# A decoder layer on one Trainium2 core: expert tiles in one pipeline instead of pairs, second norm two tiles behind

## The chip, the cores and the metric

The kernel runs on one core of a Trainium2 chip. The metric is the device time of one execution in microseconds (us). The engines are TensorE (PE; its weight loads are PEld), VectorE (DVE), ScalarE (ACT), GpSimd (POOL) and SyncE (SP, which only issues DMAs here). GpSimd issues the indirect DMAs, that gather or scatter rows by a list of row numbers; they go through a queue of their own, q0, beside the weight loads of SyncE in q1. All share the core's 16 DMA engines.

## What is computed

One layer over 576 tokens (a prompt of 512 and 8 x 8 samples) of width 1024: a mixer, a norm, a mixture of experts, a second norm.

```python
x = _layer_norm(DEEPNORM_ALPHA * x + m, ln1_g, ln1_b)         # m: pooling and short convolution, two projections
g_top, g_idx = lax.top_k(jax.nn.softmax(xf @ w_group + b_group), 1)       # 1 of 4 expert groups
e_top, e_idx = lax.top_k(jax.nn.softmax(e_in_group), 2)                   # 2 of its 8 experts
for e in range(32):
    hdn = jax.nn.silu(xf @ w1[e]) * (xf @ w3[e])              # 1024 -> 512
    acc = acc + combine[:, e:e + 1] * (hdn @ w2[e])           # 512 -> 1024
x = _layer_norm(DEEPNORM_ALPHA * x + acc, ln2_g, ln2_b)
```

All is float32. Every expert has three matrices of 2 MB (w1, w3, w2), 192 MB in all.

## The kernel before, in words

Up to some 196 us the mixer runs: projections with the weights split in two parts, the out projection, the first norm, the router's logits. Five blocks of x1 (the normed rows) stay in x_tok and are also written to x1_dram. Then VectorE computes the routing (who goes where) in a chain of small instructions, with dummy products on TensorE (`keep_warm`) in between.

Tokens are sorted into tiles of 64 slots. There are 33 tiles: one per expert, in an order held in `order`, with tile 9 (SHARED + 1) using the expert of tile 8 again, and tile 32 (E). The 64 rows of a tile are worked on as two halves of the width in 128 partitions. Per tile, TensorE does w1 and w3 (`into_hidden`, line 702, 32 products each), turns h (`turn_hidden`, 711), and multiplies by w2 (`down`, 723, 16 products). ScalarE computes silu (948) and fills ye with the tile's x1 rows (977); VectorE multiplies h_rows (1491), copies hT (1496), adds the product to ye (1502).

The first two tiles take their rows by products with a one-hot matrix (`fetch_first`, 671); from tile 2 on GpSimd gathers them from x1_dram by an indirect DMA for two tiles at once (`fetch`, 1104), and `turn_pair` (690) turns them. `token_table` (777) makes the row numbers and gates of all tiles.

Every token has two experts. Each tile t leaves its result for those tokens whose first expert it is in first_dram: `store(t)` (1082), which waits for ye. For the tokens whose second expert it is, GpSimd reloads the row left by an earlier tile into one of four `prev` buffers: `load(t)` (1086), which waits until store(t-1) has landed. VectorE then does `final(t)`: adds ye to prev (1508), computes the norm (`norm2`, 1514 to 1527, with a square root by ScalarE in `spread`, 990), and GpSimd sends the rows out: `send(t)` (1090 and 1094), which waits for final. Engines work in order; a wait holds all behind it.

Weights come in blocks of 2 MB into ten buffers (nine and tenth_block, which lies where x_tok was). `order_of_loads` gives their order; load n waits until the block that used its buffer, ten loads before, was consumed (`block_free`). The first nine need no such wait. On SyncE, loads 9 to 11 come before the wait for table_ready, then four loads of ln2, then load 12 and the others.

Before the change tiles run in pairs (`pair`): w1 and w3 of a, w1 of b, turn of a's h, w3 of b, down a, turn of b, turn of the next pair's rows, down b. On GpSimd a tile's order is store(t), send(t-1), load(t+1), and at even t a fetch. On VectorE, final(2m-1) comes after keep_hT(2m), final(2m) after keep_hT(2m+1). After pair 15 follows tile 32 alone; VectorE has final(31) before products(32).

Of the kernel before, what the change touches and what calls it, by code (L numbers as in the profile page):

```python
# [13 lines left out]
P = 128  # L14
D = 1024
# [45 lines left out]
SHARED = 8  # L61


def order_of_loads():

    loads = [(kind, t) for t in range(2) for kind in ("w1", "w3", "w2")]
    for m in range(1, PAIRS):
        tiles = [t for t in (2 * m, 2 * m + 1) if t != SHARED + 1]
        loads += [(kind, t) for t in tiles for kind in ("w1", "w3")] + [("w2", t) for t in tiles]
    return loads + [(kind, E) for kind in ("w1", "w3", "w2")]  # L70
# [31 lines left out]
def build(nc, x_prompt, x_sample, state_pool, state_conv, w_in, w_pool_map, pool_scale, conv_w, w_out,  # L102
# [3 lines left out]
    with ctx:  # L106
# [43 lines left out]
        cleared = at("cleared", MIX_AT, (ZR + 2) * DH)  # L150
# [214 lines left out]
        def _(sp):  # L365
# [44 lines left out]
            for j in range(NT):  # L410
                sp.dma_start(first_dram[j * P:j * P + ROWS[j], :], token_rows(x_prompt, x_sample, j)).then_inc(first_cleared, 16)
            sp.wait_ge(w_low, 4)
            sp.dma_start(win_a, win[:, :, 3 * DP:4 * DP]).then_inc(win_loaded[1], 16)
            sp.wait_ge(w_low, 8)
            sp.dma_start(win_b, win[:, :, DP:2 * DP]).then_inc(win_loaded[2], 16)
            sp.wait_ge(w_low, 12)
            sp.dma_start(win_a, wout[:, :, 0:512]).then_inc(wout_loaded[0], 16)
            sp.wait_ge(w_low, 16)
            sp.dma_start(win_b, wout[:, :, 512:D]).then_inc(wout_loaded[1], 16)
            sp.wait_ge(in_done, 16)  # L420
            load_in(1, w3, 0)
            load_out(2, 0)
            sp.wait_ge(in_dve, 8)
            sp.wait_ge(utail_kept, NG)
            sp.wait_ge(tail_stored, 64)
            load_out(5, 1)
            sp.wait_ge(out_done, NT)
            load_in(6, w1, 2)
            load_in(7, w3, 2)
            sp.wait_ge(out_done, 2 * NT)  # L430
            load_in(0, w1, 0)
            load_in(3, w1, 1)
            load_in(4, w3, 1)
            load_in(8, w1, 3)

# [32 lines left out]
            for n in range(EARLY_BLOCKS, 3 * EARLY):  # L468
                block_free(n)
                load(n)  # L470
# [5 lines left out]
            sp.wait_ge(order_ready, 1)  # L476
            for n in range(3 * EARLY, len(LOADS)):
                block_free(n)
                load(n)
# [13 lines left out]
        def _(pe):  # L493
# [123 lines left out]

            def route(j):
# [21 lines left out]
            for j in range(NT - 2, NT):  # L640
                route(j)
                if j + 1 < NT:
                    turn_x1(j + 1)

            def keep_warm(products):

                for _ in range(products):
                    pe.matmul(ps[:, 0, 0:P], ident[:, :], ident[:, :], start=True, stop=True)


            keep_warm(21)
# [11 lines left out]
            def fetch_first(i):  # L663
# [5 lines left out]
                for j in range(NT):  # L669
                    for g in range(2):  # L670
                        mm = pe.matmul(ps[64 * g:64 * g + 64, BX[0], :], hot_first[:, i, j, :],
                                       x_tok[:, j, g * DH:(g + 1) * DH], start=(j == 0), stop=(j == NT - 1))
# [41 lines left out]
            def down(b, loads, seq, last=False):  # L714
# [4 lines left out]
                for k in range(KF):  # L719
                    if last and k == KF // 2:  # L720
                        pe.wait_ge(last_loaded, 16)
# [5 lines left out]
            def first_pair():  # L727
# [4 lines left out]
                into_hidden("w1", 0, 16, 0, 0)  # L732
                into_hidden("w3", 1, 16, 0, 0)
                fetch_first(1)
                token_table()
                turn_first(1)
                pe.wait_ge(xeT_ready, 2)
                into_hidden("w1", 3, 16, 1, 1)
                turn_hidden(0)
                into_hidden("w3", 4, 16, 1, 1)  # L740
                down(2, 16, 0)
                turn_hidden(1)
                turn_pair(1)
                down(5, 16, 1)

            def pair(m):
                a, b = 2 * m, 2 * m + 1
                pe.wait_ge(xeT_ready, 2 * m + 2)
                into_hidden("w1", *place("w1", a), a, 0)
                into_hidden("w3", *place("w3", a), a, 0)  # L750
                into_hidden("w1", *place("w1", b), b, 1)
                turn_hidden(a)
                into_hidden("w3", *place("w3", b), b, 1)
                down(*place("w2", a), a)
                turn_hidden(b)
                turn_pair(m + 1)
                down(*place("w2", b), b)

            def last_tile():
                into_hidden("w1", *place("w1", E), E, 0)  # L760
                into_hidden("w3", *place("w3", E), E, 0)
                turn_hidden(E)
                down(*place("w2", E), E, last=True)
# [17 lines left out]

            keep_warm(12)
            first_pair()
            for m in range(1, PAIRS):
                pair(m)

            pe.wait_ge(xeT_ready, 2 * PAIRS + 2)
# [17 lines left out]
        def _(act):  # L805
# [212 lines left out]
            for m in range(1, PAIRS):  # L1018
                pair(m)
# [614 lines left out]
```

## Time and profile before

| | |
|---|---|
| median of 3 runs | 725.46 us (722.87 to 726.48) |
| profiled execution | 724.48 us, its span 722.7 us |
| TensorE busy | 609.7 us (84%) |
| VectorE, ScalarE, GpSimd busy | 306.5, 181.7, 158.3 us |
| DMA | 235.99 MB, mean 327 GB/s; q1 75.3%, q0 4.8% of the 16 engines' span |
| mean granted clock of TensorE | 0.962 |

Times in the rows are in us from the start of the span, which leaves some 1.8 us of the execution outside. Busy shares are averages over stages with different limits: the mixer to 196 us, the routing to about 240, the expert stage with its weights to about 697, and a tail. So the rows are read stage by stage.

### The profile page before, as it was taken

To read this page: it belongs to the slowest core of one execution; us is meant where nothing else is said; L and a number is where in the kernel's file an instruction comes from. 1 tells how busy PE (TensorE), PEld (TensorE's weight loads), DVE (VectorE), ACT (ScalarE), POOL (GpSimd) and SP (SyncE) were. 2 spreads that over 40 slices of the span, in tenths; PEclk is the share of its full clock that TensorE was granted. 3 is DMA by queue.
4 is the path that set the end of the run, shared out by engine and by line. 5 is a ranking of instruction groups with operands and counts; after the bars stand their busy time and mean duration, and the time that the engine had idled before them with its cause. 6 is when DMAs were issued, how large, how long until landed. Compare 5 with 4: busy or idle time off the path is not lost.

```text
span 722.7 us, 10598 instructions
## 1 busy us (share of the span) xinstructions
PE 609.7 (84%) x4220; PEld 419.2 (58%) x4220; DVE 306.5 (42%) x786; ACT 181.7 (25%) x287; POOL 158.3 (22%) x181
## 2 busy tenths in 40 slices
PE   5999999999899899799799798987777776877852
PEld 5999999878765356456445445544443534444430
DVE  4561585426584134344434343353426232323532
ACT  4232323201211223232332232223223222313210
POOL 1000000000000413343323234234132322224231
PEclk9999999999899999999999989999999999999996
DMA  9943033842668799999999999999999999999930
GB/s 268 282 159 133 2 117 117 350 189 103 246 293 349 285 418 420 418 417 416 422 415 419 414 423 417 421 418 417 422 417 424 414 426 416 424 419 416 391 135 8
DMA packets 45754, 235.99 MB, mean 327 GB/s; under 512 B 13683, under 2 KB 18291, under 8 KB 28728
## 3 DMA queue, kind: packets, MB, share of 16 engines
q1 hardware_dynamic: 32303, 220.92, 75.3%
q0 software_dynamic: 12544, 11.71, 4.8%
q10 hardware_dynamic: 857, 2.67, 0.9%
q8 instruction: 34, 0.56, 0.3%
q14 instruction: 16, 0.13, 0.0%
HBM read 237.69 MB, written 30.20 MB: 371 GB/s over the span
## 4 chain that ended last, share of the span: by engine, by line
issue 36%; SPq 18%; DMA 17%; PE 16%; POOL 9%; DVE 2%; ACT 1%; POOLq 0%; DVEq 0%
SPq L403 12%; DMA tenth_block<-in_w 12%; PE ps L543 9%; SPq L407 5%; PE ps L702 3%; DMA prev<-first_outputs,final_row 2%; POOL out L1094 2%; POOL first_outputs L1082 2%; POOL out L1090 2%; POOL prev L1086 2%; PE ps L723 2%; DMA first_outputs<-ye,first_row 2%; SPq L453 1%; DMA xe_odd<-x_rows,pair_row 1%; PE ps L506 1%
## 5 line engine op out<-in xcount | busy, mean ns | idle before, releaser
L702 PE MATMUL ps<-blocks,ln 128*64 128x256 f32 x1952 | 229.3, 391 | 54.4 <-DMA blocks<-in_w 38.7
L702 PEld LDWEIGHTS ps<-blocks,ln 128*64 128x64 f32 x1952 | 154.5, 140 | 128.6 <-issue 61.8
L723 PE MATMUL ps<-blocks,hT 128*64 128x512 f32 x464 | 109.9, 617 | 9.6 <-DMA blocks<-in_w 8.8
L1086 POOL DMA_INDIRECT prev<-first_outputs,final_row x32 | 34.4, 1076 | 234.3 <-DMA first_outputs<-ye_more,first_row 110.6
L723 PEld LDWEIGHTS ps<-blocks,hT 128*64 128x64 f32 x464 | 33.5, 141 | 68.0 <-issue 53.5
L807 ACT ACTIVATE ln<-ps 128x512 f32<-128x512 f32 (+1 forms) x38 | 20.0, 572 | 113.1 <-PE ps L690 94.2
L1496 DVE COPY hT<-ps 128x256 f32<-128x256 f32 x33 | 13.9, 421 | 71.3 <-PE ps L711 71.3
L543 PE MATMUL ps<-xT_high,w_in_high 128*128 128x288 f32 x256 | 40.6, 300 | 2.9 <-ACT w_in_high L807 1.7
L990 ACT ACTIVATE std<-rstd,eps 128x1 f32<-128x1 f32 x32 | 9.4, 295 | 123.9 <-DVEq L1523 114.3
L948 ACT ACTIVATE silu<-ps 128x256 f32<-128x256 f32 x33 | 12.7, 384 | 109.9 <-PE ps L702 105.3
L1491 DVE SCALAR_TENSOR_TENSOR h_rows<-silu,slot_gate,ps 128x256 f32<-128x256 f32 x33 | 15.7, 477 | 57.7 <-PE ps L702 57.6
L543 PE MATMUL ps<-xT_low,w_in_high 128*128 128x288 f32 x256 | 40.0, 299 | 0.0
L543 PE MATMUL ps<-xT_high,w_in_low 128*128 128x288 f32 x256 | 39.7, 298 | 0.0
L543 PEld LDWEIGHTS ps<-xT_high,w_in_high 128*128 128x128 f32 x256 | 35.8, 188 | 3.7 <-ACT w_in_high L807 1.9
L1090 POOL DMA_INDIRECT out<-prev,final_row x32 | 32.0, 1001 | 23.5 <-DVE prev L1527 14.3
L543 PEld LDWEIGHTS ps<-xT_low,w_in_high 128*128 128x128 f32 x256 | 36.5, 192 | 0.0
L543 PEld LDWEIGHTS ps<-xT_high,w_in_low 128*128 128x128 f32 x256 | 36.4, 191 | 0.0
L1094 POOL DMA_INDIRECT out<-prev,sample_row x32 | 32.0, 1001 | 9.8 <-issue 9.8
L1209 DVE TENSOR_TENSOR w_in_low<-blocks,w_in_high 128x1024 fp32r<-128x1024 f32 x16 | 19.6, 1224 | 31.7 <-ACT w_in_high L807 31.5
L1508 DVE TENSOR_TENSOR prev<-prev,ye_more 128x512 f32<-128x512 f32 x16 | 11.1, 694 | 51.2 <-DMA prev<-first_outputs,final_row 51.2
L1129 POOL MEMSET cleared<- 128x3072 f32 x1 | 2.7, 2658 | 135.5 <-DVEq L1576 135.5
L600 PE MATMUL ps<-w_out_high,mix_high 128*128 128x512 f32 (+1 forms) x80 | 31.5, 394 | 0.0
(233 smaller groups left out, 787.4 us busy)
## 6 DMA issues: line engine op xcount, KB each, us to landing
blocks<-in_w SPq DMA_DIRECT2D x86, 2048.0 KB
tenth_block<-in_w SPq DMA_DIRECT2D x9, 2048.0 KB
blocks<-in_w_in SPq DMA_DIRECT2D x3, 2048.0 KB, 10.8
blocks<-in_w_out SPq DMA_DIRECT2D x2, 2048.0 KB, 7.9
x_tok<-in_x_prompt SPq DMA_DIRECT2D x4, 512.0 KB, 5.2
blocks<-in_w_in SPq DMA_DIRECT2D x4, 512.0 KB, 10.6
first_outputs<-in_x_prompt SPq DMA_DIRECT2D x4, 512.0 KB, 8.6
x_rows<-x_tok ACTq DMA_DIRECT2D x4, 512.0 KB, 2.7
```

Source lines behind the costliest of these rows:

```text
L403: sp.dma_start(in_block(b), src.rearrange("(p c) f -> p c f", c=KD)).then_inc(block_loaded[b], 16)
L407: sp.dma_start(out_block(b).rearrange("p (g c) d -> p g c d", g=2), src.rearrange("(g p c) d -> p g c d", g=2, c=KF // 2)).then_inc(block_ ...
L543: mm = pe.matmul(ps[:, 2 * (c % 2) + h, 0:HALF], w_part[a][:, c % 2, k, :], xT[b][:, k, h * HALF:(h + 1) * HALF], start=(i == 0 and k == 0 ...
L600: mm = pe.matmul(ps[0:r, o % 4, :], mix_part[a][:, k, j * P:j * P + r], wout_part[h][b][:, k, :], start=(i == 0 and k == 0), stop=(i == 2 ...
L702: mm = pe.matmul(ps[64 * g:64 * g + 64, bank, 0:FH], x, w[:, k, g * FH:(g + 1) * FH], start=(k == 0), stop=(k == KD - 1))
L723: mm = pe.matmul(ps[64 * g:64 * g + 64, BY, :], hT[:, k % 2, k // 2 * SLOTS:(k // 2 + 1) * SLOTS], w[:, k, g * DH:(g + 1) * DH], start=(k ...
L807: return nc.scalar.activation(out, in_, ACT.Copy, **kw)
L1086: return g.indirect_dma_start(out=prev[w], out_offset=None, in_=first_rows[:, :], in_offset=rows_at(idx), bounds_check=last_row, oob_is_er ...
L1090: return g.indirect_dma_start(out=prompt_rows[:, :], out_offset=rows_at(idx), in_=prev[w], in_offset=None, bounds_check=last_prompt_row, o ...
L1094: return g.indirect_dma_start(out=sample_rows[:, :], out_offset=rows_at(idx), in_=prev[w], in_offset=None, bounds_check=last_sample_row, o ...
L1209: v.tensor_tensor(low, (win_a, win_b)[c // NG % 2][:, :, g * P:(g + 1) * P], high, ALU.subtract).then_inc(w_low, 1)
L1491: v.scalar_tensor_tensor(h_rows, silu, slot_gate[:, bass.DynSlice(seq, 1)], ps[:, B3, 0:FH], ALU.mult, ALU.mult).then_inc(h_ready, 1)
```

## The change

- `order_of_loads`: instead of six blocks per pair, per tile t: w1 and w3 of t, then w2 of t-1; from tile 30 on each tile's own w2 right after its w1 and w3.
- TensorE: one loop over tiles. Tile t does w1, turn of h of t-1, w3, at odd t the turn of the next pair's rows, down of t-1. From tile 30 on a tile also turns and multiplies down its own h. The first tiles: `token_table` before the second `fetch_first`, the turn of h of tile 0 inside that, the turn of tile 1's rows inside down(0).
- Dummy products: 4 and 2 new ones around the last two routes, 15 instead of 21, 2 instead of 12.
- SyncE: order_ready is waited for after load 10, table_ready and ln2 come after load 12.
- VectorE: the `order` is computed right after products(0); final(t-2) comes first in tile t's part, then keep_hT(t-1), products(t), add_y(t-1).
- ScalarE: spread(t-2), silu_of(t), then the pair's copies at odd t.
- GpSimd: clears xe_odd, fetches 1, clears prev, fetches 2; then per tile send(t-2), load(t-1), store(t-1), and at even t a fetch.

```diff
+STAGGERED = E - 2
...
+    for t in range(E + 1):
+        loads += [(kind, t) for kind in ("w1", "w3")]
+        loads += [("w2", s) for s in ([t - 1] if t < STAGGERED else [t - 1, t] if t == STAGGERED else [t]) if s >= 0]
+    return [(kind, t) for kind, t in loads if t != SHARED + 1]
...
-            for n in range(EARLY_BLOCKS, 3 * EARLY):
+            for n in range(EARLY_BLOCKS, EARLY_BLOCKS + 2):
+                block_free(n)
+                load(n)
+            sp.wait_ge(order_ready, 1)
+            for n in range(EARLY_BLOCKS + 2, EARLY_BLOCKS + 4):
                 block_free(n)
                 load(n)
             sp.wait_ge(table_ready, 1)
...
+            pe.wait_ge(out_kept, NT + 3)
+            keep_warm(4)
+            route(NT - 2)
+            turn_x1(NT - 1)
+            keep_warm(2)
+            route(NT - 1)
...
-            keep_warm(21)
+            keep_warm(15)
...
-                into_hidden("w1", 0, 16, 0, 0)
-                into_hidden("w3", 1, 16, 0, 0)
-                fetch_first(1)
+                into_hidden("w1", *place("w1", 0), 0, 0)
+                into_hidden("w3", *place("w3", 0), 0, 0)
                 token_table()
-                turn_first(1)
+                fetch_first(1, lambda: turn_hidden(0))
+                down(*place("w2", 0), 0, lambda: turn_first(1))
                 pe.wait_ge(xeT_ready, 2)
+                into_hidden("w1", *place("w1", 1), 1, 1)
+                into_hidden("w3", *place("w3", 1), 1, 1)
+                pe.wait_ge(table_ready, 1)
                 turn_pair(1)
...
+            def tile(t):
+
+                if t % 2 == 0:
+                    pe.wait_ge(xeT_ready, t + 2)
+                into_hidden("w1", *place("w1", t), t, t % 2)
+                if t <= STAGGERED:
+                    turn_hidden(t - 1)
+                into_hidden("w3", *place("w3", t), t, t % 2)
+                if t % 2:
+                    turn_pair((t + 1) // 2)
+                if t <= STAGGERED:
+                    down(*place("w2", t - 1), t - 1)
...
-            keep_warm(12)
-            first_pair()
-            for m in range(1, PAIRS):
-                pair(m)
+            keep_warm(2)
+            first_tiles()
+            for t in range(2, E + 1):
+                tile(t)
+                if t >= STAGGERED:
+                    turn_hidden(t)
+                    down(*place("w2", t), t, last_half if t == E else None)
...
+            for t in range(2, E):
+                if t > 2:
+                    spread(t - 2)
+                silu_of(t)
+                if t % 2:
+                    keep_xeT((t + 1) // 2)
+                    fill_pair((t + 1) // 2)
+            spread(E - 2)
+            spread(E - 1)
             silu_of(E)
...
-            g.memset(cleared[:, :], 0.0).then_inc(prev_cleared, 1)
+            g.memset(xe_odd[:, :, :], 0.0).then_inc(prev_cleared, 1)
             pool.wait_ge(prev_cleared, 1)
             pool.wait_ge(x1_stored, 16 * NT)
             fetch(1)
+            g.memset(prev_mem[:, :, :], 0.0).then_inc(prev_cleared, 1)
+            fetch(2)
             pool.wait_ge(first_cleared, 16 * NT)
             store(0)
...
-            for t in range(2, E - 1):
-                store(t)
-                send(t - 1)
-                if t < E - 2:
-                    load(t + 1)
+            pool.wait_ge(prev_cleared, 2)
+            for t in range(2, E):
+                if t > 2:
+                    send(t - 2)
+                load(t - 1)
+                store(t - 1)
                 if t % 2 == 0 and t // 2 + 2 <= PAIRS:
                     fetch(t // 2 + 2)
+            load(E - 1)
             store(E - 1)
-            load(E - 1)
             send(E - 2)
             load(E)
             send(E - 1)
...
             products(0)
+            swapped(iota[0:1, 0:E], by_place[0:1], moved[0:1])
+            v.tensor_copy(order[0:1, :], by_place[0:1]).then_inc(order_ready, 1)
...
-            for m in range(1, PAIRS):
-                products(2 * m)
-                keep_hT(2 * m)
-                final(2 * m - 1)
-                products(2 * m + 1)
-                add_y(2 * m % YR, 2 * m)
-                keep_hT(2 * m + 1)
-                final(2 * m)
-                add_y((2 * m + 1) % YR, 2 * m + 1)
+            for t in range(2, STAGGERED + 1):
+                if t > 2:
+                    final(t - 2)
+                keep_hT(t - 1)
+                products(t)
+                add_y((t - 1) % YR, t - 1)
+            keep_hT(E - 2)
+            add_y((E - 2) % YR, E - 2)
+            final(E - 3)
+            products(E - 1)
+            keep_hT(E - 1)
+            add_y((E - 1) % YR, E - 1)
+            final(E - 2)
             final(E - 1)
             products(E)
```

## Rows read from the trace of the kernel before

**Rows 1.** Busy time by stage: length, PE, PEld, DVE, ACT, POOL, clock, DMA, GB/s.

```profile
253.00:672.00 419.00, 346.74 (x2480) 202.62 (x2476) 156.12 (x450) 109.44 (x171) 130.69 (x127) 0.97 1.01 419
550.00:672.00 122.00, 91.56 (x652) 54.39 (x648) 40.32 (x114) 29.48 (x47) 35.48 (x35) 0.99 1.01 419
```

**Rows 2.** Timeline of SyncE: start, length, what was issued, how often.

```profile
241.08 9.49 SPq L403 DMA_DIRECT2D blocks<-in_w  x4
```

**Rows 3.** Timeline of all engines at the last tile; in brackets the wait before.

```profile
702.28 0.47 DVE L1491 SCALAR_TENSOR_TENSOR h_rows<-silu,slot_gate,ps 128x256 f32<-128x256 f32 x1
702.64 1.01 POOL L1090 DMA_INDIRECT out<-prev,final_row  x1 [5.17 <-DVE prev L1527]
...
704.12 5.62 PE L723 MATMUL ps<-blocks,hT 128*64 128x512 f32 x16 [0.61 <-DVE hT L1496]
```

**Rows 4.** Timeline of GpSimd: stores (1082) and reloads (1086).

```profile
252.26 1.02 POOL L1082 DMA_INDIRECT first_outputs<-ye,first_row  x1 [0.30 <-issue]
266.85 1.03 POOL L1086 DMA_INDIRECT prev<-first_outputs,final_row  x1 [13.57 <-DMA first_outputs<-ye,first_row]
...
331.21 1.05 POOL L1086 DMA_INDIRECT prev<-first_outputs,final_row  x1 [5.67 <-DMA first_outputs<-ye_more,first_row]
...
386.21 1.05 POOL L1086 DMA_INDIRECT prev<-first_outputs,final_row  x1 [4.56 <-DMA first_outputs<-ye_more,first_row]
...
498.66 1.05 POOL L1086 DMA_INDIRECT prev<-first_outputs,final_row  x1 [5.89 <-DMA first_outputs<-ye_more,first_row]
...
690.69 1.05 POOL L1086 DMA_INDIRECT prev<-first_outputs,final_row  x1 [1.07 <-DMA first_outputs<-ye_more,first_row]
```

**Rows 5.** Waits from 250 to 670: who, for whom, us in total, times, longest.

```profile
POOL prev L1086 <- DMA first_outputs<-ye_more,first_row: 107.5, 14, 12.2
```

**Rows 6.** Timeline of TensorE: dummies, first gather, table, a down, three blocks.

```profile
203.82 2.94 PE L648 MATMUL ps<-ident 128*128 128x128 f32 x24
206.70 4.51 PE L671 MATMUL ps<-x_tok,hot_first 128*64 128x512 f32 x20
...
224.65 2.79 PE L777 MATMUL ps<-io 128*64 128x153 f32 x40
...
236.41 3.60 PE L723 MATMUL ps<-blocks,hT 128*64 128x512 f32 x16
...
250.03 10.53 PE L702 MATMUL ps<-blocks,ln 128*64 128x256 f32 x96
```

**Rows 7.** Timeline of VectorE: last input of the table, and the order.

```profile
218.84 0.42 DVE L1478 TENSOR_TENSOR io<-io,gates 128x255 f32<-128x255 f32 x1
...
234.31 0.17 DVE L1568 CAST order<-io 1x32 int32<-1x32 f32 x1
```

**Rows 8.** A stretch of TensorE: length, busy, clock, DMA share, GB/s.

```profile
196.00:197.00 1.00, 1.00 (x11) 0.50 1.08 455
```

**Rows 9.** Timeline: GpSimd's first fetch and TensorE, which waits for it.

```profile
239.57 1.22 POOL L1104 DMA_INDIRECT xe_odd<-x_rows,pair_row  x1 [0.29 <-POOL cleared L1129]
...
243.92 0.48 PE L690 MATMUL ps<-ident,xe_odd 128*128 128x128 f32 x1 [3.47 <-DMA xe_odd<-x_rows,pair_row]
```

**Rows 10.** Timeline of VectorE: a whole final, and starts after a wait for prev.

```profile
261.37 0.68 DVE L1508 TENSOR_TENSOR prev<-prev,ye 128x512 f32<-128x512 f32 x1
...
265.21 0.75 DVE L1527 SCALAR_TENSOR_TENSOR prev<-prev,rstd,ln 128x512 f32<-128x512 f32 x1
...
273.38 0.69 DVE L1508 TENSOR_TENSOR prev<-prev,ye_more 128x512 f32<-128x512 f32 x1 [4.21 <-DMA prev<-first_outputs,final_row]
...
340.88 0.69 DVE L1508 TENSOR_TENSOR prev<-prev,ye_more 128x512 f32<-128x512 f32 x1 [2.76 <-DMA prev<-first_outputs,final_row]
...
394.72 0.69 DVE L1508 TENSOR_TENSOR prev<-prev,ye_more 128x512 f32<-128x512 f32 x1 [2.01 <-DMA prev<-first_outputs,final_row]
...
697.75 0.69 DVE L1508 TENSOR_TENSOR prev<-prev,ye_more 128x512 f32<-128x512 f32 x1 [9.39 <-DMA prev<-first_outputs,final_row]
```

**Rows 11.** DMA queues from 290 to 510 us: packets, MB, share of 16 engines.

```profile
q0 software_dynamic: 6322, 6.04, 8.1%
```

## What the change does to the time, predicted from these rows

> **What bounds the kernel now.** I read the stages first, then who waited for whom, then the timelines of GpSimd and VectorE. The stages [rows 1] say that the expert stage is fed at the limit of the DMA engines: share 1.01 from 253 to 672 us, about 419 GB/s, while TensorE stands idle for 17% of that stretch and 25% of its last part, 550 to 672. So weights set the time as long as nothing else falls behind them. From the issue of the thirteenth block (241.08 [rows 2], call it n = 12, as LOADS does) to the last landing near 697 us, 84 blocks come in: 5.4 us each, 16.2 us for a tile with three blocks. After them stands a tail: the last down product starts at 704.12 [rows 3] and the span ends at 722.7, 18.6 us later.
>
> The second thing to see is how far behind the weights the products run. With ten block buffers TensorE may lag by some nine blocks before the stream stops. It does lag at first, and catches up: the reloads of GpSimd at 386.21 and 498.66 [rows 4] are eight tiles apart, 14.1 us a tile, less than 16.2. What sets these 14.1 us is not TensorE (24.6 us of products a pair) but GpSimd's own order of waits: it stands 107.5 us in 14 waits for stores to land before it may issue the reload of a row [rows 5], and as much again for the stores of the other ye buffers. This chain is long but short enough.
>
> **The start, part by part.** The 42 dummy matmuls of the first call end 0.65 us after the mask is there; 30 end before it. The second call's 24 take 2.94 us and push the first gather to 206.70 [rows 6]; four of them take 0.5, and the gather then waits only for hot_first (near 204.0). Gain: 2.6 us, to w3 of tile 0 (220.5 to 217.9). The table now comes first. Its inputs are complete with the last product of line 1478 (219.26 [rows 7]), less the 0.6 gained at the mask: 218.7. With 2.8 us for the table [rows 6] it is done at 221.5, and the order, which moves ahead of the row arithmetic, near 223.5 instead of 234.5 [rows 7]. The second gather, with one turn of h in it, then ends at 226.5 instead of 224.8; h is turned and copied by 226.9, down(0) with the turn of tile 1 in its middle ends at 231.2 (it took 3.6 from 236.41 before [rows 6]), w1 of tile 1 at 234.8, w3 at 238.4 (3.5 a block [rows 6]). Block n = 12 now waits for that w1, not for down(0): it is issued at 234.8 instead of 241.08 [rows 2]. From there the engines were full before, so **the weight stream moves 6.3 us forward**. The table's four loads of ln2 hide beside it.
>
> Fewer dummies may lower the clock: it was granted at 0.50 in 196 to 197 [rows 8] (1.2 GHz) after a stretch of 1 us without products. Four new dummies lie exactly there, so I take zero; the other end is that a gather of 4.5 us runs at half clock, 4.5 us at most. Below nothing is possible too: if the new dummies keep the clock up where it was halved, up to 1 us. GpSimd clears 1024 columns instead of 3072 before its first fetch, and table_ready comes near 229, so the first fetch is in before it is wanted (239.57 plus 4.3 us before [rows 9]). Its first store moves from 241.64 to 237.3.
>
> **The pipeline.** The products per tile are the same (about 12.2 us: two blocks, one down, turns). What is new is the order of GpSimd: send(t-2), load(t-1), store(t-1). Here the reload for the second norm of tile t-1 is queued behind send(t-2), and that waits for final(t-2). Before, load(t+1) stood behind send(t-1): the norm of one tile released the reload for the norm two tiles on. Now it releases that of the next tile. So there is a **loop once per tile**: final(t-2) on VectorE, its two sends, the reload, its landing, final(t-1). Its length:
> - final: 261.37 to 265.96, 4.6 us [rows 10]
> - from its end to the first send 0.27 (the final of 697.75 [rows 10] ends at 702.36, its send starts at 702.64 [rows 3]), two sends of 1.31 each: 2.9 us
> - issue to landing of the reload: sixteen reloads have VectorE waiting for them, so their landing is seen: first 266.85 to 273.38, last 690.69 to 697.75 [rows 4, 10]; 6.5 to 9.7 (331.21 to 340.88), 8.5 at 386.21 (in at 394.72); the mean of the sixteen is 8.1.
>
> Sum 15.6 us. VectorE works in order: behind final(t-2) it has keep_hT(t-1), products(t) and add_y(t-1), and TensorE waits for the first of these with down(t-1). So TensorE goes at 15.6 us a tile where it went at 14.1 and could go at 12.2, and never catches up with the weights. Nothing of the reload is hidden, although "two tiles behind" gives final more room: the room is in the place of final, not in the issue of its reload.
>
> The first turn of the loop: store(0) issued 237.3 behind a fetch. The store at 252.26 [rows 4], behind a reload and a fetch, had landed 14.4 us later (the reload at 266.85 waited for it); less one reload, 2.8 (a third of the 8.5 us from 386.21 to 394.72, in which two sends queued before it and the reload passed), 11.6 us: 249. Reload 6.5 (the one with nothing ahead): final(1) starts at 255. Then final(28), in tile 30, starts at 255 + 27 x 15.6 = 676.2. The stream could have given it at 641: lag 28 us in terms of down, within the 42 us that ten buffers allow (nine blocks of 5.4, less a block's own issue), so the DMA stays full and the weights are all in by 691.
>
> **The tail.** final(29) at 691.8, reload of 30 issued 7.5 later at 699.3, then store(30) at 700.6. From here the DMA is nearly empty: landings between 4.3 (239.57 [rows 9]) and 7.0 (690.69 [rows 4]); I take 6, and 6.5 for the store, since the last ones of before were still near 7 at a low share. Reload 31 issued 707.3, in at 713.3, final(31) ends 717.9. It still stands in front of products(32) in VectorE's order, as before, so handling the last three tiles singly frees nothing in this case. products(32) 718.0; from there to down 1.8 (702.28 to 704.12 [rows 3]), 719.8; from down to the end 18.6 [rows 3]: **738.4**. The profiled execution has 724.48 for a span of 722.7, 1.8 more, and the median of the runs, 725.46, is 1.0 above it: 738.4 + 2.8 = **741.2 us**.
>
> Every microsecond of the loop counts 27 times. The forecast stands on 8.1 us of landing, and moves with it: 7.5 gives 725, 8.5 gives 752.
>
> **Rivals.**
> 1. *The loop is shorter than the stream's pace and the stream ends it.* That needs less than about 14.4 us a tile, a landing below 6.9. For it: the lone reload took 6.5, and an unloaded fetch 4.3 [rows 9]. Against it: the mean of sixteen beside a full stream. Time: weights 6.3 us earlier; w3 of tile 32 ends at 691.0 instead of 697.3; final(31) is then done, since store(30) is some ten microseconds earlier, so products(32) starts at 691.0 instead of 702.28 less 6.3 for the stream, 5.0 more; down(32) 692.8, end 711.4, or 709.4 at full clock (it ran 5.6 us at 0.64 instead of 3.65). Time 713. Chance 0.22.
> 2. *In between*, landing 6.9 to 7.6: 715 to 729. Chance 0.15, half of it within 0.5% of before.
> 3. *The software queue makes it worse.* This ends on the slow side with its own mechanism: the queue of GpSimd serves its packets one after the other beside the weights, 6322 in 220 us with 16 tiles in them [rows 11], so 13.75 us of service per tile, nearly always busy. In the loop the queue lies empty when the sends come and three transfers must pass then: 6.5 for the first, 2.8 for each other, 12.1 from the first send, where my sum has 2.6 + 8.1 = 10.7. Loop 17.0. It decides as soon as the loop exceeds 16.2: the lag grows from 28 to its limit of 42, the stream then pauses, which shortens the landings again. Time 741 + 14 = 755, up to 760. Chance 0.18.
>
> A rule of the Trainium skill speaks for the first rival: "DMA: Bandwidth & Descriptors", section "Anatomy of one DMA — SWDGE (gpsimd) path", gives a transfer issued by GpSimd a fixed cost of about 2.0 us plus its bytes at 436 GB/s. By it a reload of at most 256 KB would be in after some 2.6 us (an estimate from that page), the loop would be 10.1 us and the stream would set the time, 713 us. The trace does not agree beside full weight traffic (8.1 us), and comes only near it where there was little (4.3 us).
>
> **How the numbers follow.** Forecast (loop 15.2 to 16.0, 729 to 752) 0.45, rival 1 0.22, rival 2 0.15, rival 3 0.18. The predicted time is the forecast's, 741. The range reaches down into rival 1 (713, start and tail uncertain by 2) and up to 760. A measurement of this kernel tells about 0.5% from no change, 3.6 us. Faster than 721.8: 0.22 + 0.07 = 0.29; within: 0.08; slower: 0.63.
>
> **What would show it.** In the changed trace: starts of line 1508 at an even distance of 15 to 16 us from 255 on, each with a wait for its reload; GpSimd waits for VectorE (final) before its sends rather than for stores; TensorE waits for hT before each down and nearly never for blocks; n = 12 issued near 235; the DMA share falls before 700 while products go on to 727. It is wrong if GpSimd's reload lands within 7 us of its issue, if VectorE doesn't wait for prev, or if TensorE waits for blocks in the second half as before.

## The result and the profile after

The changed kernel takes 764.2 us (median of 4 runs, 763.93 to 764.56) against 725.8 for the one before: a ratio of 1.054, 95% interval 1.051 to 1.057. It is slower, as forecast, but by 38 us instead of 15, and 4 us above the upper end of the range. One execution of a kernel named below, the profiled one of e8, was disturbed (740.3 us, where the other nine lie at 729 to 738): it is left out of e8's median, and its trace is used for landings only.

Busy time by stage (length, then PE, PEld, DVE, ACT, POOL, clock, DMA share, GB/s), to be laid beside [rows 1]:

```profile
350.00:400.00 50.00, 46.26 (x318) 24.93 (x316) 17.45 (x49) 17.41 (x24) 17.28 (x17) 0.92 0.72 278
400.00:550.00 150.00, 114.67 (x752) 62.48 (x750) 50.28 (x144) 44.09 (x60) 40.28 (x40) 0.90 1.01 420
550.00:670.00 120.00, 98.10 (x656) 54.89 (x652) 39.42 (x113) 37.60 (x52) 32.76 (x33) 0.90 1.00 412
```

The weights still come at the full rate, except from 350 to 400 us, where the DMA engines are busy for 0.72 of the time: my reading is that the ten buffers were full, since TensorE waits for no block there. That stretch costs the stream 0.28 x 50 = 14 us. Who waited for whom, 250 to 720 us (us in total, times, longest), beside [rows 5]:

```profile
POOL out L1089 <- DVE prev L1525: 231.1, 28, 11.1
DVE prev L1506 <- DMA prev<-first_outputs,final_row: 151.2, 26, 7.9
PE ps L731 <- DVE hT L1494: 97.3, 26, 5.9
```

GpSimd waited for stores before; now it waits 28 times for a final (line 1525 is its last step). VectorE waits 26 times for a reload, and TensorE 26 times for the turned h that stands behind the final on VectorE. The view has no row of TensorE waiting for weights. The chain that ended last passes through one turn (start, length, what):

```profile
407.63 0.99 POOL out L1089
408.62 0.30 issue
408.92 0.99 POOL out L1093
409.91 0.31 issue
410.22 12.52 DMA prev<-first_outputs,final_row
422.76 0.70 DVE prev L1506
...
427.29 0.43 DVE hT L1494
427.85 6.45 PE ps L731 x16
```

Two sends, the reload and its landing, and the final are the loop of the prediction; its next send was issued at 427.65, 0.3 us after that final. Turned h and the down product hang off the final. They are on this chain because it comes back to GpSimd through the store; they are no part of the loop. The first reload's final starts at 253.65, that of tile 28 at 703.66: 450.0 us for 27 turns, 16.67 a tile. The reloads whose landing VectorE waited for took 9.5 us in the mean (26 of them), where the sum had 8.1. In between, from the start of a final to the issue of the reload, it was 7.49 us (27 tiles), where the sum had 7.5.

The start, on TensorE, beside [rows 6], and SyncE's issue of block n = 12, beside [rows 2]:

```profile
203.02 4.51 PE L679 MATMUL ps<-x_tok,hot_first 128*64 128x512 f32 x20 [0.23 <-DVE hot_first L1406]
...
217.62 2.84 PE L779 MATMUL ps<-io 128*64 128x153 f32 x40 [0.76 <-DVE io L1476]
```

```profile
233.74 0.34 SPq L404 DMA_DIRECT2D blocks<-in_w  x1
```

### The profile page after: what moved, and what is told of

It reads as the page before. It is cut to its first block, busy times and chain, and to the rows that moved or that the text cites. A ratio compares the mean times of both kernels' runs of the same rounds, so it can differ in the third digit from the quotient of the medians.

```text
span 762.2 us, 10589 instructions
## 1 busy us (share of the span) xinstructions
PE 633.5 (83%) x4200; PEld 418.7 (55%) x4200; DVE 307.4 (40%) x786; ACT 218.7 (29%) x317; POOL 156.8 (21%) x182
## 4 chain that ended last, share of the span: by engine, by line
PE 34%; issue 24%; DMA 19%; DVE 13%; POOL 8%; ACT 1%; DVEq 0%; POOLq 0%; ACTq 0%
DMA prev<-first_outputs,final_row 17%; PE ps L547 13%; PE ps L731 10%; PE ps L604 6%; POOL out L1093 2%; POOL out L1089 2%; POOL first_outputs L1081 2%; PE ps L710 1%; DVE prev L1522 1%; DVE stats L1512 1%; DVE prev L1506 1%; DMA first_outputs<-ye,first_row 1%; PE ps L633 1%; PE ps L510 1%; POOL prev L1085 1%
## 5 line engine op out<-in xcount | busy, mean ns | idle before, releaser
L731 PE MATMUL ps<-blocks,hT 128*64 128x512 f32 x496 | 152.7, 770 | 95.2 <-DVE hT L1494 95.1
L710 PE MATMUL ps<-blocks,ln 128*64 128x256 f32 x1888 | 215.1, 381 | 1.5 <-ACT ln L809 1.5
L710 PEld LDWEIGHTS ps<-blocks,ln 128*64 128x64 f32 x1888 | 140.6, 137 | 74.5 <-issue 16.1
L731 PEld LDWEIGHTS ps<-blocks,hT 128*64 128x64 f32 x496 | 48.1, 176 | 181.4 <-issue 181.0
L1500 DVE TENSOR_TENSOR ye<-ye,ps 128x512 f32<-128x512 f32 x16 | 11.0, 688 | 77.9 <-PE ps L731 77.9
L1500 DVE TENSOR_TENSOR ye_more<-ye_more,ps 128x512 f32<-128x512 f32 x16 | 11.0, 688 | 73.3 <-PE ps L731 73.3
L1506 DVE TENSOR_TENSOR prev<-prev,ye 128x512 f32<-128x512 f32 x15 | 10.4, 692 | 70.3 <-DMA prev<-first_outputs,final_row 70.2
## 6 DMA issues: line engine op xcount, KB each, us to landing
blocks<-in_w_in SPq DMA_DIRECT2D x3, 2048.0 KB, 10.7
```

Of the source, the lines that this page charges most:

```text
L710: mm = pe.matmul(ps[64 * g:64 * g + 64, bank, 0:FH], x, w[:, k, g * FH:(g + 1) * FH], start=(k == 0), stop=(k == KD - 1))
L731: mm = pe.matmul(ps[64 * g:64 * g + 64, BY, :], hT[:, k % 2, k // 2 * SLOTS:(k // 2 + 1) * SLOTS], w[:, k, g * DH:(g + 1) * DH], start=(k ...
L1500: v.tensor_tensor(ye[u], ye[u], ps[:, BY, :], ALU.add).then_inc(y_kept, 1)
L1506: in_order(v.tensor_tensor(prev[w], prev[w], ye[u], ALU.add))
```

## The experiments

All times are medians, and each ratio is to runs of the kernel before on the same chip; that kernel gave 726.1 beside e1 to e4, 727.4 beside e5 to e8, 726.9 beside e9 to e11. Each kernel has one trace. The theory was the loop; the rivals were a queue that is simply overfull, the single tiles themselves or TensorE's clock, and, within the loop, what makes a landing as long as it is.

**e2: the loop alone, in the kernel before.**

```diff
-                store(t)
-                send(t - 1)
-                if t < E - 2:
-                    load(t + 1)
+                send(t - 1)
+                load(t)
+                store(t)
```

(fetch(2) also moves ahead of load(1), and the calls behind the loop follow the new order.)

> The kernel before with only GpSimd's order changed to send(t-1), load(t), store(t), so that it too has the loop once per tile; pairs, start and tail stay as they were. Theory: 745 to 770 us, VectorE waits for prev in nearly every tile with 16 to 17 us from one to the next. Rival (the pipeline of single tiles or TensorE's lower clock is the cause): 726 us as before.

Measured: 765.5 us, 1.053 of before (1.049 to 1.057), the same as the changed kernel. Its waits:

```profile
POOL out L1090 <- DVE prev L1525: 281.7, 26, 14.7
...
DVE prev L1506 <- DMA prev<-first_outputs,final_row: 196.4, 26, 13.8
```

Pairs, the old start, the old dummies and the old tail are all in it. GpSimd's order is enough for the whole loss.

**e1: the reload ahead of the sends, in the changed kernel.**

```diff
-                if t > 2:
-                    send(t - 2)
                 load(t - 1)
+                if t > 2:
+                    send(t - 2)
                 store(t - 1)
```

> The changed kernel with one line moved: GpSimd issues load(t-1) before send(t-2), so no reload waits for a norm any more. Theory (loop of final, two sends, reload, landing, once per tile, 16.7 us a tile in the changed kernel): the loop is gone, the weight stream sets the time, 710 to 722 us, VectorE waits for prev in few tiles. Rival (GpSimd's queue has so much to serve that the order does not matter): 755 to 765 us.

Measured: 745.1 us, 1.024 (1.022 to 1.027). It fits neither expectation. The first loop is gone, but a second one shows in GpSimd's timeline:

```profile
435.62 1.05 POOL L1085 DMA_INDIRECT prev<-first_outputs,final_row  x1 [11.42 <-DMA first_outputs<-ye,first_row]
436.98 1.02 POOL L1089 DMA_INDIRECT out<-prev,final_row  x1 [0.31 <-issue]
438.30 0.99 POOL L1093 DMA_INDIRECT out<-prev,sample_row  x1 [0.30 <-issue]
439.60 0.99 POOL L1081 DMA_INDIRECT first_outputs<-ye,first_row  x1 [0.30 <-issue]
440.89 1.05 POOL L1103 DMA_INDIRECT xe_odd<-x_rows,pair_row  x1 [0.30 <-issue]
451.23 1.01 POOL L1085 DMA_INDIRECT prev<-first_outputs,final_row  x1 [9.29 <-DMA first_outputs<-ye,first_row]
```

The reload waits until store(t-2) has landed, and that store was issued 4 us after the previous reload, behind it and two sends, and took 11.6 us. So reload to reload is 15.6 here; the finals come every 16.0 us. The waits of this kernel put 283.6 us (148.9 and 134.7, 15 each) on GpSimd waiting for stores. Here the landing of a reload, issued 6 to 13.5 us after the transfer ahead of it, was 8.2 us, near the 8.1 of the prediction.

**e5: GpSimd's order of the kernel before, in the changed kernel.**

```diff
-                if t > 2:
-                    send(t - 2)
-                load(t - 1)
-                store(t - 1)
+                store(t - 1)
+                if t > 2:
+                    send(t - 2)
+                load(t)
```

(load(1) is issued after store(0), and the load(E - 1) behind the loop falls away.)

> The changed kernel with GpSimd's order of the kernel before: store(t-1), send(t-2), load(t), so that a reload is issued two tiles before its norm and a norm releases the reload of the next tile but one. Theory (GpSimd's order alone is what costs): neither the loop over the sends (after: 16.7 us a tile) nor the one over the stores of e1 (15.9) is left; 14 us a tile as in the kernel before until the stream is reached, 711 to 720 us. Rival (single tiles and the two norms behind cost by themselves, by TensorE's clock or by VectorE's order): 740 or more.

Measured: 717.5 us, 0.987 of before (0.983 to 0.991). As the theory had it, 47 us below the changed kernel and 1.3% below the kernel before. Its timeline of GpSimd:

```profile
435.38 1.05 POOL L1085 DMA_INDIRECT prev<-first_outputs,final_row  x1 [5.93 <-DMA first_outputs<-ye,first_row]
436.73 1.12 POOL L1103 DMA_INDIRECT xe_odd<-x_rows,pair_row  x1 [0.31 <-issue]
443.49 1.43 POOL L1081 DMA_INDIRECT first_outputs<-ye_more,first_row  x1 [5.64 <-DVE ye_more L1500]
445.22 1.01 POOL L1089 DMA_INDIRECT out<-prev,final_row  x1 [0.30 <-issue]
446.54 1.39 POOL L1093 DMA_INDIRECT out<-prev,sample_row  x1 [0.30 <-issue]
452.21 1.05 POOL L1085 DMA_INDIRECT prev<-first_outputs,final_row  x1 [4.29 <-DMA first_outputs<-ye_more,first_row]
```

Load(t) now follows send(t-2), and its norm, final(t), comes two tiles later: the norm of one tile no longer holds up the norm of the next. The DMA share is 1.01 from 550 to 670 and the clock 1.00 there:

```profile
550.00:670.00 120.00, 90.78 (x632) 52.00 (x632) 41.49 (x118) 39.16 (x54) 37.32 (x36) 1.00 1.01 419
```

TensorE is idle for 24% of it, as in [rows 1]: it has caught up, and the weights set the time again.

**What makes the landing long: e3, e4, e8, e11, e10.** In e3 GpSimd pauses between the sends and the reload:

```diff
+                for _ in range(4):
+                    g.memset(logits[:, :, :], 0.0).then_inc(pause, 1)
+                    paused[0] += 1
+                    pool.wait_ge(pause, paused[0])
                 load(t - 1)
```

> The changed kernel with four small fills on GpSimd between the two sends and the reload of each tile, about 1 us together (to be read from the trace). Theory of the loop: every us in it counts once per tile, so 20 to 32 us more per us of pause, less where the starved stream makes landings shorter. Rival (the service of the queue is the limit, issue times do not count): within 5 us of 764.

Measured: 768.5 us (1.056, 1.053 to 1.059), the rival's figure. The pause lengthened the way from a final's start to the reload from 7.5 to 8.9 us, by 1.4, but the landing fell from 9.5 to 8.1, and the turns hardly changed (16.77 against 16.67). Counted from the first send the landing was the same (12.1 and 12.2; in tiles 15 to 28 alone, 11.5 in both). So a reload issued 1.4 us later still landed as far behind the first send. The sum of the prediction counted issue and landing as independent terms; they are not.

e4 moves one send behind the reload:

```diff
                 if t > 2:
-                    send(t - 2)
+                    send_one(t - 2)       # to y_prompt
                 load(t - 1)
+                if t > 2:
+                    send_other(t - 2)     # to y_sample
```

> The changed kernel with the send to y_sample issued behind the reload instead of ahead of it. If what stands ahead in GpSimd's queue is what makes the landing long (about 2.8 us of service a transfer), the loop loses 1.3 us of issue and 2.8 us of queue: 12.5 to 13 us, less than the stream's pace, 712 to 725 us. If the landing is the reload's own time beside the weights, only the 1.3 us of issue: 730 to 740 us.

Measured: 730.2 us (1.004, 1.001 to 1.007), 15.3 us a tile. That is the lower end of the second expectation: little more is gained than the 1.3 us of issue. The landing counted from the reload's own issue was 9.2 us, against 9.6 in the changed kernel.

e8 leaves the sends to y_sample out:

```diff
                 send_prompt(w, final_row[:, t:t + 1]).then_inc(final_stored[w], 16)
-                send_sample(w, sample_row[:, t:t + 1]).then_inc(final_stored[w], 16)
```

> The changed kernel without the sends to y_sample, so that y_sample is not written at all (in the tiles up to 32) and GpSimd's queue has one transfer less per tile. e4, which only moved them, still has 15.5 us a tile. If the service of the queue is what the reload waits for: 12 us from first send to landing become about 9.3, a loop near 14.2, 711 to 722 us. If the reload's own time beside the weights counts, as the prediction had it: the same 15.5 us as e4 and 728 to 735 us.

Measured: 731.2 us (1.005, 1.003 to 1.007); the rival's figure. Leaving a send out is worth no more than moving it behind the reload, so it is not the total service of the queue that counts here but what is issued ahead of the reload within the turn.

e11 leaves out the other one:

```diff
-                send_prompt(w, final_row[:, t:t + 1]).then_inc(final_stored[w], 16)
                 send_sample(w, sample_row[:, t:t + 1]).then_inc(final_stored[w], 16)
```

> The changed kernel without the sends to y_prompt (y_prompt is not written in the tiles up to 32), the counterpart of e8, which left out the sends to y_sample. Eight ninths of the rows are the prompt's. From the runs so far a reload lands 8.1 us after its issue with nothing just ahead (e1), 10.9 us after the first send with the prompt's send ahead (e4, e8), 12.0 with both (after, e3). If what counts is the rows that stand ahead (2.8 us for the prompt's send, 1.1 for the sample's): 9.2 us from the send to the landing, a loop of 14.1 us and 712 to 722 us. If every transfer costs the same whatever it moves: the loop of e8, 15.6 us, and 731 us.

Measured: 727.7 us (1.002, 1.000 to 1.005), 15.1 us a tile. Nearly the loop of e8, though the send that is left has an eighth of the rows of the other:

```profile
510.21 0.98 POOL L1093 DMA_INDIRECT out<-prev,sample_row  x1 [9.96 <-DVE prev L1524]
511.50 1.05 POOL L1085 DMA_INDIRECT prev<-first_outputs,final_row  x1 [0.30 <-issue]
```

```profile
520.92 0.69 DVE L1505 TENSOR_TENSOR prev<-prev,ye_more 128x512 f32<-128x512 f32 x1 [4.35 <-DMA prev<-first_outputs,final_row]
```

10.7 us from the send to the landing. The reading by rows falls: as the transfer directly ahead, an indirect send of 128 row numbers costs the reload much the same, whether one ninth or eight ninths of the tokens' rows are in it.

e10 adds a third one, into a spare tensor:

```diff
                 send_sample(w, sample_row[:, t:t + 1]).then_inc(final_stored[w], 16)
+                g.indirect_dma_start(out=spare_rows[:, :], out_offset=rows_at(final_row[:, t:t + 1]), in_=prev[w], ...)
```

> The changed kernel with a third send per tile, a copy of the prompt's rows into a spare tensor in DRAM, between the sample's send and the reload. If transfers ahead in GpSimd's queue are served one after the other: 2.8 us more from first send to landing (14.8 instead of 12.0), a loop of 19 us where the weights flow, and, as the ten buffers then run dry more often, 785 to 840 us. If only a wait of the issuing engine counts, as with the pause of e3: about 764 to 772 us.

Measured: 789.8 us (1.085, 1.081 to 1.089), within the range given for the queue. But the third send's own issue puts 1.3 us more into each turn, and the second expectation left that out, so the time does not tell the two apart. One turn of it on GpSimd with the landing of its reload, 14.3 us from the first send, and the stage after 300 us:

```profile
506.90 1.00 POOL L1090 DMA_INDIRECT out<-prev,final_row  x1 [5.67 <-DVE prev L1528]
508.21 0.98 POOL L1094 DMA_INDIRECT out<-prev,sample_row  x1 [0.30 <-issue]
509.49 0.99 POOL L1123 DMA_INDIRECT spare_rows<-prev,final_row  x1 [0.30 <-issue]
510.79 1.05 POOL L1086 DMA_INDIRECT prev<-first_outputs,final_row  x1 [0.30 <-issue]
```

```profile
521.17 0.69 DVE L1509 TENSOR_TENSOR prev<-prev,ye 128x512 f32<-128x512 f32 x1 [9.62 <-DMA prev<-first_outputs,final_row]
```

```profile
300.00:400.00 100.00, 80.37 (x518) 42.39 (x520) 35.25 (x101) 32.56 (x46) 36.61 (x36) 0.85 0.80 317
```

The landings of this kernel are of two kinds. From the first send to the landing it is 15.0 us in the mean of the even tiles 16 to 28, and 9.2 in the odd tiles 15 to 27. The stretches of tile 16 and of tile 17, and the final of tile 17, whose first send was issued at 526.05:

```profile
506.00:521.00 15.00, 11.54 (x86) 6.75 (x84) 2.12 (x4) 5.93 (x9) 5.03 (x5) 0.98 1.01 421
525.00:535.00 10.00, 8.74 (x46) 4.17 (x48) 2.25 (x4) 2.36 (x3) 5.60 (x6) 0.72 0.94 357
535.09 0.69 DVE L1509 TENSOR_TENSOR prev<-prev,ye 128x512 f32<-128x512 f32 x1 [2.25 <-DMA prev<-first_outputs,final_row]
```

The long landings stand where the DMA engines are full, the short ones where the stream is a little below that. An even tile also has a fetch behind the store of the turn before. No run separates the two. The mean in the table mixes both kinds.

Together, from the timelines (mean over the reloads of tiles 2 to 28 that VectorE waited for; turns are those from the first to the 28th final; the sum is 4.6 for the final, 0.3 to the first send, and the landing counted from that send). The landing is given from the reload's own issue too:

| kernel | just ahead of the reload | own issue to landing | first send to landing | sum | turn | us |
|---|---|---|---|---|---|---|
| e1 | nothing | 8.2 | | | 16.0, other loop | 745.1 |
| e11 | sample | 8.9 | 10.35 | 15.2 | 15.1 | 727.7 |
| e8 | prompt | 9.4 | 10.65 | 15.5 | 15.5 | 731.2 |
| e4 | prompt | 9.2 | 10.5 | 15.4 | 15.3 | 730.2 |
| e2 | both | 8.9 | 11.45 | 16.3 | 16.4 | 765.5 |
| e3 | both, then a pause of 1.4 | 8.1 | 12.1 | 17.0 | 16.8 | 768.5 |
| after | both | 9.6 | 12.2 | 17.1 | 16.7 | 764.2 |
| e10 | three | 9.0 | 12.9 | 17.8 | 17.35 | 789.8 |

The sum meets the turn within 0.2 us in four kernels; in after, e3 and e10 the measured turn is 0.2 to 0.45 shorter, since these ran the buffers full at times and then had short landings, some of which VectorE did not wait for (at most 3.85 and 4.8 us for tiles 7 and 9 in after).

What makes the landing long is left open in part. Of the step from one send ahead to two, 1.3 us is the issue of the second send; from the reload's own issue one send and two look alike (8.9 to 9.4, and 8.9 to 9.6). So two readings fit: a queue served in order, and a reload that takes about a microsecond more when it is issued directly behind a send, however many. E3 fits both, since its pause also parts the reload from the send. What all traces have in common is the price of the place: 8.1 to 8.2 us with a pause behind the sends (e3, e1), 8.9 to 9.6 directly behind one.

**The start and the tail: e7, e9, e6**, each on top of e5. e7 has the old dummies (21 and 12, none around the routes).

> e5 with the dummy products of the kernel before (21 and 12, none around the routes). By the prediction's sum the first gather starts 2.6 us later and so the stream: 2 to 3 us more than e5. If the clock profits from them, or the start is hidden behind a later wait, within 1 us of e5.

Measured: 720.7 us (0.991, 0.989 to 0.994), 3.1 more than e5, as expected, though the two intervals overlap. Block n = 12 is issued 2.5 us later than in e5 (235.80):

```profile
238.28 0.34 SPq L404 DMA_DIRECT2D blocks<-in_w  x1
```

This one profile proves little by itself: the same instruction stands at 233.7 in after and at 238.8 in e3, which have the same start; executions differ by that much at the end of the mixer.

e9 has the table behind the second gather:

```diff
-                token_table()
-                fetch_first(1, lambda: turn_hidden(0))
+                fetch_first(1)
+                token_table()
+                turn_hidden(0)
                 down(*place("w2", 0), 0, lambda: turn_first(1))
```

> e5 with the token table behind the second gather again and the turn of tile 0's h behind the table. By the prediction's sum for the start the hidden rows of tile 0 come 4 to 5 us later, so w1 of tile 1 ends and block n = 12 is issued near 238 instead of 234, and the stream ends that much later: 3 to 5 us more than e5. Rival (the start is hidden by the later catching up of TensorE, as its lag is not at the buffers' limit): within 1 us of e5.

Measured: 722.5 us (0.994, 0.993 to 0.996), 4.9 more than e5; in the ratios 0.8% or 5.5 us, outside both intervals.

```profile
241.54 0.34 SPq L404 DMA_DIRECT2D blocks<-in_w  x1
```

It is issued 5.7 us after that of e5. Where the stream sets the time, the start counts in full. The rival that a lag of TensorE hides it falls.

e6 puts the last tile's products ahead of the last but one final:

```diff
-            final(E - 1)
             products(E)
             keep_hT(E)
+            final(E - 1)
```

(and on ScalarE silu_of(E) before spread(E - 1)).

> e5 with products(32) and keep_hT(32) ahead of final(31) on VectorE, and silu of tile 32 ahead of the root of tile 31 on ScalarE. If final(31) still holds up the last products as before (5 us there), 3 to 6 us less than e5; if the reload of tile 31 is in early in single tiles, as rival 1 of the prediction has it, no change to e5 within 1 us.

Measured: 717.3 us (0.987, 0.983 to 0.992), 0.2 below e5. In the profiled executions it is 3.2 us (span 713.9 against 717.1). About 1.2 us of that is the order: in e5 the last products start 1.3 us after the last block's product ends (695.75), since they wait for silu behind the root of final(31), and in e6 0.1 us after it. The last block's product itself came 1.65 us later in e5 than in e6 (692.08 against 690.43).

```profile
697.09 0.48 DVE L1489 SCALAR_TENSOR_TENSOR h_rows<-silu,slot_gate,ps 128x256 f32<-128x256 f32 x1 [0.35 <-ACT silu L950]
```

Four runs each can't tell 1 us from none. This stays open.

## Why the prediction was right and wrong, point by point

**The bound and the loop: right.** That VectorE's final, two sends, the reload and its landing follow each other once per tile, that TensorE waits for h behind it and that GpSimd's order alone does this, is shown by e2, which has nothing else of the change, and by e5, which has all of the change but this.

**The start: right in its parts, with luck in the match.** First gather 203.0 (204.1 expected), block n = 12 at 233.7 (234.8), final(1) at 253.7 (255). But the same start put the gather at 208.1 and the block at 238.8 in e3, so that one execution agrees within 1.3 us is luck. What counts is e9 and e7, which show the parts at 5 and 3 us. The new dummies did not keep the clock up: it was granted at 0.50 from 195 to 197 in after too, as in [rows 8]. The gather of after ran at full clock (4.51 us, as in [rows 6]), so the price of zero held there. But in two of the ten traces with this start, e5 and e8, the gather took 6.2 us, in e5 with a clock granted at 0.50 from 206 to 208. That 1.7 us lies inside the bound of 4.5 that the prediction gave.

**The landing: wrong, and it is the whole miss.** The sum had 4.6 + 2.9 + 8.1 = 15.6 us a turn; measured were 16.67, which makes 28.8 us more over 27 turns. The start gave 1.3 of it back and the way from the 28th final to the end 3.7 (58.5 us against 62.2), which leaves the 23.8 us between the span of 762.2 and the one summed. The step that failed is taking 8.1 us, the mean of sixteen landings of the kernel before, for a reload in another position. In its place the landing measured 9.6 us where VectorE waited for it, and 9.2 over all of tiles 2 to 28, 1.1 more than summed; the rest of the turn was as summed. In the kernel before a reload was issued when a store had just landed. All of the sixteen but the first, which has no send before it, stand 5.3 to 13.2 us behind the last send (9 in the mean), as the one of 386.21 in [rows 4] behind this send:

```profile
380.67 0.99 POOL L1094 DMA_INDIRECT out<-prev,sample_row  x1 [0.30 <-issue]
```

In the changed kernel it is 1.3 us. Directly behind one send or two a reload takes 8.9 to 9.6 us from its own issue to its landing.

**Rival 3: near by luck in part.** It had 12.1 us from the first send, measured 12.2, and I gave it 0.18. But it was built from 6.5 us for the first transfer and 2.8 for each other: 6.5 with nothing ahead, 9.3 with one send. Measured were 8.2 and 10.4 to 10.7. Two errors of opposite sign met at two sends, and e2, also with two, had 11.45. Its price was too low as well: 755 to 760, since a pause of the stream would shorten the landings and so end itself. The stream paused for long once, and lost 14 us, which that price, the growth of the lag alone, doesn't have. Two landings were short then. The next five turns took 18.1 us in the mean, and the last fourteen 16.4, near the stream's 16.2. That the lost stream explains the difference is argued from this one trace.

**The tail: half right.** final(31) did stand before products(32); in after the last products waited for silu behind it. The last down again ran long (5.59 us at a granted 0.62; 5.62 in [rows 3]). What singling the last three tiles out is worth no run tests.

**Rival 1** fell for the changed kernel, and with it the figure of the Trainium skill ("DMA: Bandwidth & Descriptors", "Anatomy of one DMA — SWDGE (gpsimd) path"): about 2.0 us plus the bytes, against 8.2 us measured beside full weight traffic with nothing ahead. Only where the stream paused or had ended do landings come near it (at most 3.85 us for tile 7 of after, 2.9 for tile 32 of e10). Its time, 713, is about what the kernel gives once the loop is gone (717.5 in e5).

**TensorE's clock.** With 3.7 us of idling in the mean before a down (97.3 us in 26 waits) the clock fell in the stage, 0.90 against 0.97 in [rows 1], and the down at 407.83, behind 4.97 us of idling, took 6.2 us at a granted 0.58 instead of 3.65. The loop doesn't contain a product, so this should cost nothing; that is argued, not tried.

## What to carry to other kernels

In a pipeline of waits look for the chain that closes once per turn: an engine's own program order (here "send, then reload" on GpSimd) can tie the next turn's input to this turn's output, though each buffer has room for four. Moving the consumer later gives no room if the issue of what it consumes stays behind its predecessor; issue the reload for the turn after next instead. And a transfer's duration belongs to its place in the queue: take it from rows with the same things directly ahead. Here 1.1 us in that one term, 27 times over, was more than the forecast's whole difference of 15 us.

## What the runs showed of the hardware

- A reload by GpSimd's queue beside full weight traffic (about 419 GB/s) lands 8.2 us after its issue when the transfer ahead was issued 6 us or more before it (e1). Directly behind one send it is 8.9 to 9.4 (10.4 to 10.7 from that send; e11, e4, e8), behind two 8.9 to 9.6 (11.45 in e2 and 12.2 in after, from the first).
- Behind three sends it is 15.0 us from the first send in the even tiles 16 to 28 of e10, and 9.2 in the odd ones, where the DMA share was 0.92 to 0.94 in the four stretches that were read: a small gap in the weight traffic goes with landings of 9 us instead of 15.
- How many of the 128 row numbers of the transfer ahead lead to a row hardly matters: 10.35 us with the sends to y_sample, one ninth of the tokens' rows (e11), 10.65 with the sends to y_prompt, the other eight (e8).
- Delaying the issue of the reload by 1.4 us behind two sends did not delay its landing (12.1 in e3 against 12.2 in after, from the first send).
- Executions of the same start differ by some 5 us at the end of the mixer (the first gather at 203.0 in after, at 208.1 in e3), more than the parts of the start that were tested; only medians of ratios tell those.
